# Two diffusion trunk layers: three of the four norms leave the input of the matmul and go to its output, and GpSimd splits each weight tile in two halves

## The reference

```
def rmsnorm(x, g):      return x * rsqrt(mean(x * x, axis=-1) + EPS) * g
def adaln(cvec, w, b):  return split(silu(cvec) @ w + b, 6)
def modulate(x, g, shift, scale):
    return rmsnorm(x, g) * (1 + scale) + shift
def conv_ffn(h, w_up, conv_w, conv_b, w_down):
    u = dwconv_centered(h @ w_up, conv_w, conv_b)
    g, v = split(u, 2)
    return (silu(g) * v) @ w_down
h = modulate(x, norm_mix_g, shift, scale);  x = x + gate * mixer(h)
h = modulate(x, norm_ffn_g, shift, scale);  x = x + gate * conv_ffn(h, ...)
```

## Time and profile before

| | us |
|---|---|
| median of 3 runs (range) | 2111.81 (2111.33 to 2116.29) |
| profiled execution, its own time | 2114.69 |
| its span | 2112.9 |
| mean granted clock of PE, share of full | 0.954 |

### The profile page before, as it was taken

How to read it: one execution, slowest core, us unless ns; L and a number is a source line. 1 busy time by engine, 2 the same in 40 slices (tenths; PEclk the granted TensorE clock), 3 DMA queues, 4 the chain that set the end, 5 groups by cost and what they waited for, 6 DMA issues and landing times. The chain is left out here.

```text
span 2112.9 us, 32465 instructions
## 1 busy us (share of the span) xinstructions
PE 1954.0 (92%) x12945; PEld 1826.9 (86%) x12945; DVE 1022.0 (48%) x1456; ACT 582.7 (28%) x1046; POOL 1123.4 (53%) x437
## 2 busy tenths in 40 slices
PE   5799888899999999997999999987897999999997
PEld 3688777789999899997998989976896999999997
DVE  2545673454414432537467676668315451452343
ACT  2233330121101110213365655655102210220121
POOL 2223324445575567764544445432474777776763
PEclk8799998899999999998999999988898999999999
DMA  9321118645525222222333333311421222222211
GB/s 285 103 60 40 36 37 265 184 142 181 161 82 182 91 60 76 66 77 90 103 118 93 97 116 98 110 60 50 130 70 40 79 70 70 79 69 71 79 55 75
DMA packets 293060, 208.78 MB, mean 99 GB/s; under 512 B 7480, under 2 KB 285021, under 8 KB 292445
## 3 DMA queue, kind: packets, MB, share of 16 engines
q1 hardware_dynamic: 292957, 207.32, 32.2%
HBM read 196.63 MB, written 10.67 MB: 98 GB/s over the span
## 5 line engine op out<-in xcount | busy, mean ns | idle before, releaser
L825 POOL TENSOR_SCALAR w_hi<-raw 128x1024 fp32r<-128x1024 f32 (+1 forms) x216 | 607.9, 2814 | 945.3 <-PE ps L856 870.6
L856 PE MATMUL ps<-h_hi,w_hi 128*128 128x322 f32 (+1 forms) x2304 | 560.5, 325 | 22.0 <-DVE h_lo L1679 22.0
L856 PE MATMUL ps<-h_lo,w_hi 128*128 128x322 f32 (+1 forms) x2304 | 533.2, 313 | 0.0
L856 PE MATMUL ps<-h_hi,w_lo 128*128 128x322 f32 (+1 forms) x2304 | 532.3, 312 | 0.0
L828 POOL TENSOR_TENSOR w_lo<-raw,w_hi 128x1024 fp32r<-128x1024 f32 (+1 forms) x216 | 515.1, 2385 | 18.0
L856 PEld LDWEIGHTS ps<-h_hi,w_hi 128*128 128x128 f32 x2304 | 391.8, 192 | 51.3 <-issue 34.0
L856 PEld LDWEIGHTS ps<-h_hi,w_lo 128*128 128x128 f32 x2304 | 393.5, 191 | 0.0
L856 PEld LDWEIGHTS ps<-h_lo,w_hi 128*128 128x128 f32 x2304 | 391.7, 191 | 0.0
L856 PE MATMUL ps<-g_hi,w_hi 128*128 128x322 f32 (+1 forms) x816 | 191.1, 316 | 10.2 <-DVE g_lo L1923 10.2
L856 PE MATMUL ps<-g_lo,w_hi 128*128 128x322 f32 (+1 forms) x816 | 189.4, 314 | 0.0
L856 PE MATMUL ps<-g_hi,w_lo 128*128 128x322 f32 (+1 forms) x816 | 188.8, 313 | 0.0
(11 more groups left out here) (291 smaller groups left out, 2208.5 us busy)
## 6 DMA issues: line engine op xcount, KB each, us to landing
ada<-in_ada_w SPq DMA_DIRECT2D x48, 1024.0 KB, 5.9
raw<-in_ffn_w_up SPq DMA_DIRECT2D x88, 512.0 KB, 3.8
raw<-in_ssd_w_in SPq DMA_DIRECT2D x40, 512.0 KB, 4.0
R<-scr_acs SPq DMA_DIRECT2D x40, 512.0 KB, 4.8
raw<-in_ffn_w_down SPq DMA_DIRECT2D x32, 512.0 KB, 4.1
raw<-in_att_w_in SPq DMA_DIRECT2D x16, 512.0 KB, 5.9
raw<-in_ssd_w_out SPq DMA_DIRECT2D x16, 512.0 KB, 4.2
raw<-in_ffn_w_down SPq DMA_DIRECT2D x16, 384.0 KB, 3.4
```

Of the source, the lines that this page charges most:

```text
L825: nc.gpsimd.tensor_scalar(w_hi[j % 2][:, 0:k, :], raw[j][:, 0:k, :], 1.0, None, ALU.mult).then_inc(w_hi_done, 1)
L856: ins = mm(out[:, cols], w[slot][:, k, :], x[:, k_of(k), cols], start=first and k == 0 and i == 0, stop=last and k == n - 1 and i == 2)
```

## The change

Four edits.

1. For norms 0, 1 and 3 the root leaves h. `high` and `low` write h_hi = round(x·gain) and h_lo = x·gain − h_hi straight behind each residual, with no root in them. Since the root is one number per token (a column of the tile), it is multiplied into the accumulator when a tile is evicted: `root_row` and `row` put it into a row buffer (`rbs`, `rrow_att`), and `scale` multiplies a whole MLP tile in place in PSUM; in attention the multiplication is the copy to SBUF itself. The shift goes into the two columns that were zero, now side by side (`PADS`): the matmul turns them into W·shift, and ACT adds that as a bias. In the MLP, `side_pads` copies them to the tile's borders for the outer taps, and a small operation forms the biases. `ss` and `norm_rb` stand inside the first two tiles behind the norm.
2. Norm 2 (state-space) stays as it was.
3. POOL makes each weight tile with four instructions, two halves of `w_hi` and two halves of `w_lo`, instead of two.
4. The modulation steps come in another column order (`ADA_ORDER`), so that gains come first; the last ones of the attention output are done two tiles earlier. h of norm 3 has its own memory (`h2_a` to `h2_d`), since its old place still holds the state-space output. The residual loop behind the state-space mixer is unrolled.

```diff
-                pool.wait_ge(w_hi_done, t + 1)
-                nc.gpsimd.tensor_tensor(w_lo[j % 2][:, 0:k, :], raw[j][:, 0:k, :], w_hi[j % 2][:, 0:k, :].bitcast(F32),
-                                        ALU.subtract).then_inc(w_split, 1)
+                cuts = ((0, k // 2), (k // 2, k))
+                for a_, b_ in cuts:
+                    nc.gpsimd.tensor_scalar(w_hi[j % 2][:, a_:b_, :], raw[j][:, a_:b_, :], 1.0, None, ALU.mult
+                                            ).then_inc(w_hi_done, 1)
+                for n_, (a_, b_) in enumerate(cuts):
+                    pool.wait_ge(w_hi_done, 2 * t + (1 + n_))
+                    ins = nc.gpsimd.tensor_tensor(w_lo[j % 2][:, a_:b_, :], raw[j][:, a_:b_, :],
+                                                  w_hi[j % 2][:, a_:b_, :].bitcast(F32), ALU.subtract)
+                ins.then_inc(w_split, 1)
...
+                            begins = peeled and p == 0
+
+                            def row(k, half=half):
+                                if half == 0 and k == 5:
+                                    ss(n_)
+                                if half == 1 and k == 3:
+                                    norm_rb(n_)
+
+                            steps(half, half, h_of(n_), range(KD), ready=h_wait(n_) if begins and half == 0 else None,
+                                  after=row if begins else None).then_inc(mm_done, 1)
                             if ada:
                                 s = 2 * i + (s0 + half)
...
+            def high(n, k):
+
+
+                act.wait_ge(gain_done, k // 2 + 1 + 4 * n if n < 2 else 7 + n)
+                hi, _ = h_at_k(n, k)
+                for s_, cols in SEGS:
+                    ins = A_(hi[:, cols], xT[:, k, cols], ACT.Copy, scale=gain1[:, n, k, s_:s_ + 1])
...
-                            A_(buf[:, :], acc(half), ACT.Identity, bias=param_at(m + bcol),
-                               scale=param_at(m + (wc + 44))).then_inc(ffn_id, 1)
+                            for s_, cols in ((0, slice(0, S0)), (1, slice(S0, W))):
+                                b_ = 24 + 2 * half + s_
+                                ins = A_(buf[:, cols], acc(half)[:, cols], ACT.Identity, bias=small[:, b_:b_ + 1],
+                                         scale=param_at(m + (wc + 44)))
+                            ins.then_inc(ffn_id, 1)
...
+            def low(n, k):
+
+                dve.wait_ge(gain_done, k // 2 + 1 + 4 * n if n < 2 else 7 + n)
+                dve.wait_ge(h_hi_done, 8 * n + k + 1)
+                hi, lo = h_at_k(n, k)
+                for s_, cols in RANGES:
+                    ins = stt(lo[:, cols], xT[:, k, cols], gain1[:, n, k, s_:s_ + 1], f32(hi[:, cols]), ALU.mult,
+                              ALU.subtract)
+                    (step(ins) if s_ == 0 else ins.then_inc(h_ready, 1))
+
...
+            def root_row(n):
+
                 inv_root(n)
-                if n in (0, 3):
-                    h_zeros()
                 tt(diag[:, :, :], bc(ident, 1, CHUNKS), bc(small[:, 48:53], 2, P), ALU.mult).then_inc(diag_done, 1)
+
+            def row(n):
+
+                if n:
+                    step(nc.vector.memset(rrow(n)[:, PADS], -1.0))
...
-                        low(k - 1)
-                low(KD - 1)
+                for s_, cols in RANGES:
+                    step(cp(rrow(n)[:, cols], bank(4, P) if s_ == 0 else bank(5)))
+                step.wait()
+
+            def scale(slot, n):
+
+                step(tt(acc(slot), acc(slot), rrow(n)[:, :], ALU.mult))
+                step.wait()
+
+            def side_pads(slot):
+
+                step(cp(acc_wide(slot)[:, 0:W + 2:W + 1], acc(slot)[:, PADS]))
 
...
                         continue
-                    if t >= 12:
+                    src = acc(t % 2)
+                    if t < 12:
+                        h, i = divmod(t, 3)
+                        dve.wait_ge(mm_done, t + 1)
+                        if t == 0:
+                            dve.wait_ge(x_spilled, 16)
+                            row(0)
+                        if h and i == 1:
+                            dve.wait_ge(*att_end(("trk", h - 1)))
+                        if h and i == 2:
+                            dve.wait_ge(*att_end(("trv", h - 1)))
+                        tt((q_raw, k_raw, v_raw)[i][:, :], src, rrow_att[:, :], ALU.mult).then_inc(acc_free_dve, 1)
+                        if t == 0:
+                            att_zeros()
...
@@ -1904,11 +2052,19 @@
                     def pair(i, ada):
                         for half, buf in enumerate((cg, cv)):
                             m = i + (m0 + FT * half)
+                            dve.wait_ge(mm_done, 2 * i + (tp + half + 1))
+                            if isinstance(i, int) and (p, i, half) == (0, 0, 0):
+                                row(n_)
+                            scale(half, n_)
+                            side_pads(half)
+                            nw = nws[:, m:m + 1] if isinstance(m, int) else nws[:, bass.ds(m, 1)]
+                            ts(small[:, 24 + 2 * half:26 + 2 * half], acc(half)[:, PADS], nw, pcol_at(m + bc_), ALU.mult,
+                               ALU.add).then_inc(ffn_v, 1)
                             dve.wait_ge(ffn_id, 2 * i + (2 * f0 + half + 1))
...
+            for m in range(KD):
+                dve.wait_ge(mm_done, T_O + 4 * (m // 2) + 2 + m % 2 + 1)
+                buf = tn[m % 2]
+                for s_, cols in RANGES:
+                    ins = stt(buf[:, cols], acc(m % 2)[:, cols], modc(1, 2, m, s_), rbs[:, cols], ALU.mult, ALU.mult)
+                    (step(ins) if s_ == 0 else ins.then_inc(acc_free_dve, 1))
+                dve.wait_ge(acc_free_dve, dve_accs(A_O) + m)
+                for s_, cols in RANGES:
+                    ins = tt(xT[:, m, cols], xT[:, m, cols], buf[:, cols], ALU.add)
+                    (step(ins) if s_ == 0 else ins.then_inc(so_x, 1))
+                dve.wait_ge(so_x, m + 1)
+                if m:
+                    low(3, m - 1)
+                if m >= 2:
+                    add_square(3, m - 1, sq[(m - 1) % 2])
             add_square(3, 7, sq[1])
-            norm(3)
+            low(3, 7)
+            dve.wait_ge(shift_hi, 4)
```

More of the change, by code:

```diff
@@ L262, in build @@
         wdt_lo = fixed("wdt_lo", [P, KD, 64], F32R)
+        dtb_bc = fixed("dtb_bc", [P, 64])
+        a_bc = fixed("a_bc", [P, 64])
         early_end = top[0]
@@ L358, in build @@
         xdt = a("xdt", [P, 2, 512])
-        xw = [a(f"xw{i}", [P, 512]) for i in range(2)]
+        xw_1 = a("xw1", [P, 512])
         st_b = a("st_b", [P, 4, 512])
@@ L643, in _ @@
                 load(t, t, w_att[:, :, att_col(t):att_col(t) + P])
-            for s in range(5, 9):
+            for s in range(5, 8):
                 ada(s)
@@ L846, in _, with steps @@
             mm, tr = nc.tensor.matmul, nc.tensor.transpose
-            def steps(t, slot, aslot, x_hi, x_lo, ks, k_of=lambda k: k, first=True, last=True, n=KD, ready=None):
+            def steps(slot, aslot, x_of, ks, first=True, last=True, n=KD, ready=None, after=None):
                 out = acc(aslot)
@@ L1050, in _ @@
                     begin(T_B + m, A_B + m)
-                    steps(T_B + m, m % 2, m % 2, g_hi, g_lo, range(KD)).then_inc(mm_done, 1)
+                    steps(m % 2, m % 2, g_of, range(KD)).then_inc(mm_done, 1)
                 for s in ADA_B[m]:
@@ L1098, in down @@
                             ready = (lambda k: pe.wait_ge(f_ready, FT * l + m0 + k + 1)) if peeled and half == 0 else None
-                            steps(t, half, half, g_hi, g_lo, range(n), n=n, ready=ready).then_inc(mm_done, 1)
+                            steps(half, half, g_of, range(n), n=n, ready=ready).then_inc(mm_done, 1)
                     down(0, True)
@@ L1118, in y_part @@
                         pe.wait_ge(*acc_free(A_O + half - 2))
-                    ins = steps(None, half, half, y_hi, y_lo, (k % KD,), k_of=lambda _: k, first=part == 0,
-                                last=part == 1)
+                    ins = steps(half, half, y_of(part), (k % KD,), first=part == 0, last=part == 1)
                     if k % KD == KD - 1:
@@ L1263, in so_pair @@
                             pe.wait_ge(acc_free_dve, 2 * i + (half + dve_accs(A_O) - 2))
-                        steps(None, half, half, y_hi, y_lo, range(KD), k_of=lambda k: 8 * part + k, first=part == 0,
-                              last=part == 1).then_inc(mm_done, 1)
+                        steps(half, half, y_of(part), range(KD), first=part == 0, last=part == 1).then_inc(mm_done, 1)
             for k in range(12, 16):
@@ L1482, in _ @@
             ffn(0, T_F0, T_F0)
-            norm(2)
+            root(2)
+            for k in range(KD):
+                act.wait_ge(t_done, k + 1)
+                for s_, cols in SEGS:
+                    ins = A_(h_hi[:, k, cols], tn[k % 2][:, cols], ACT.Identity, bias=modc(1, 0, k, s_))
```

(17 more changed lines are left out.)

409 lines of the change are left out of this document (234 added, 175 removed).

## The result

The changed kernel takes 2078.04 us (median of 4 runs, 2075.3 to 2081.86) against 2111.98 in the same rounds: a ratio of 0.9834, with a 95% interval from 0.9815 to 0.9853 (the ratio is the recorded one; the two medians alone give 0.9839, inside the interval). The profiled execution took 2075.3 of its own time against 2114.69, with a span of 2073.5 instead of 2112.9: 39.4 less, where I had forecast 38.6.

A forecast was written before the change was run, and what follows sets the result against it. PE was taken as the bound, busy 1954.0 of 2112.9 us. The terms -16.3, -15.7, -11, +2.6, +1.5, +1.3 and -1 sum to -38.6: 2114.7 becomes 2076.1, median 2073, range 2060 to 2088.

The forecast's parts named there:

- Norm 3: Behind the state-space output: PE's third tile starts at T+20.8 (T: last tile's end) instead of 37.1, -16.3 us.
- Norm 1: Behind the attention output: PE's third tile starts at T+19.1 (T: last tile's end) instead of 34.8, -15.7 us.
- Norm 0: At the kernel's start: the second tile is done at 76.5 us instead of 87.6, -11 (7 to 12).
- MLP eviction: MLP loops: DVE's chain frees the slot at 12.9 us, PE wants it at 14.2; 0 over 44 pairs.
- g_lo: Last pair ahead of a down-projection: g_lo, which PE awaits, comes 0.5 us later; five waits, +2.6.
- Attention: Attention: 12 tiles evicted by DVE and biased by ACT, bounds 0 and +14, taken as +1.5 us; halved splits change nothing.
- State-space: Two splits each 0.5 us longer and three small instructions ahead of the first residual, +1.3; shorter DVE waits on w_lo, -1.
- The signs: Expected waits: sums about 12 us, h_lo about 6; clock near 1.0 behind norms 1 and 3; scale 0.8 to 0.9.
- attention on the path: Rival: all 12 attention evictions stay on PE's path, +14 us instead of +1.5, giving 2085; chance 0.12.
- the late waits: Rival: squares and last low part come a whole w_lo later at each norm; gains 12, 12, 7, giving 2085; chance 0.09.
- More is won: Rival: state-space and attention gain 4 us each from shorter locks, the start 12, giving about 2063; chance 0.12.
- The slow one: Rival: DVE bounds the MLP if scale costs over 0.65 us more; at 2.3 each, 2140 us; chance 0.04.

The follow-up runs named there:

- The repetition: The changed kernel run again as it is, no edit, in the same rounds as the other runs: 2080.49 us, 0.9834 of the kernel before.

## Why the prediction held, point by point

- **Norm 3** (-16.3) won 18.1. The sums were 1.2 less late (wait 0.49, not 1.7), since the additions ran beside w_lo's two halves, 2.65 us for the pair (with whole splits the wait is 1.36), and the slot wait was 1.7, not 2.
- **Norm 1** (-15.7): the third tile at T+18.2, forecast 19.1. The rest of the 18.8 in the table is mostly the modulation work that has moved.
- **Norm 0** (-11): 11.2. DVE reads the first step out at 34.49 instead of 38.88, 4.4 earlier (forecast 3.7), and the column sums take 2.3 of it back; but PE then waits 1.1 for the weights of a step and 0.9 for DVE, which I had not priced, and the last turn starts only 0.3 earlier (56.60 against 56.94). Tile 0 starts at 58.42 where I had 58.8.
- **MLP eviction** (0 in the loops) held, with its chain: evicted at 4.6 (forecast 4.6), hm at 6.3 (6.5), g_lo at 8.6 (8.3), slot free at 13.2 (12.9). The scale takes 0.831 on average, 0.89 forecast. What the step left out is the new memory of h: rows of 648 cost 1.9 us.
- **The median**: the profiled execution was forecast within 0.8 us (2076.1, measured 2075.3). The median is 5 above the 2073 given, because I took it to lie 2.9 below the profiled execution, as in the kernel before; here it lies 2.7 above. That is a matter of which execution was profiled, and no mechanism.
- **g_lo** (+2.6): the waits rose by 1.2 only; the clock took 6.0 us behind them against 3.0 before, which I had not priced. The repetition, with the same waits, lost 2.5, so this is chance.
- **Attention** (+1.5) failed in its sign: 5.8 are won by v and 7.3 by the first output matmul in this execution. The eviction by DVE, for which the +1.5 stood, costs PE no wait (12.4 us of standing still before and after). "DVE and POOL take turns and end at about the same time, so nothing" failed: the halves take 1.7 us out of PE's waits in both kernels. The other 4 us up to v are PE's busy time, that is the clock, and vary by as much between executions of the same code.
- **State-space** (+1.3 and -1): +1.3 from the last MLP residual (-28.2) to the last state-space residual (-27.0), where the sum had 0.3. The two waits for w_lo rose by 2.0 (8.9 to 10.9); that shorter locks would win 1 back does not show, since PE stands still for 2 us more with halves in this part.
- **Left out altogether:** SP's order at the attention output. I had read the diff's `ada(8)` behind `g_ready` and costed nothing; PE waits there 10.5 us instead of 1.5, and that took more than attention had won. And the last turn of the modulation, 5.3 us won, which I had put into "another column order".
- **The signs.** Scale at 0.83, hm at 1.6 (I had 1.8), the clock of 1.00 behind both norms and no wait on scale or taps inside the loops came as written. For the waits I had given about 12 on the sums and about 6 on h_lo, and 6.9 and 3.3 came: norm 2's own wait for h_lo was 3.3 already before, not 6, and on the sums only 6.4 belong to the norms that did not change.

The rivals: attention on the path and the late waits did not come. "More is won" gave attention and state-space 4 each from shorter locks: in PE's waits attention won 1.7 and state-space lost 2, and the sum did not come. The slow one is further away than I wrote: DVE has 1.8 us of cover per pair, not 1.3. The total was close because +9.0 (DMA order), +1.9 (rows) and +3.0 (clock) stand against -9 in attention and -5.3 (the turn), none of them in the sum: the mechanisms of the three norms were right, the precision of the sum was luck.

The lock rule (the Trainium skill, "SBUF — State Buffer", Who interferes with whom), which the page states not for any GpSimd operation but for one that reads SBUF, as w_hi's does, would have g_lo wait for the whole first half of w_hi that starts with it: 1.49 and its own 0.83. Here g_lo starts at 1664.60, 0.02 behind that half, and takes 1.27, so it lost 0.44: more than the nothing that I had taken from the earlier trace rows, less than the rule says. The scale at 1665.80, which reads one operand from PSUM, runs inside the same pair of w_hi in 0.82, undelayed. The earlier trace rows was thin ground: that addition overlaps w_hi for its last 0.27 us alone. The kernel before has better rows:

```profile
278.76 2.77 POOL L825 TENSOR_SCALAR w_hi<-raw 128x1024 fp32r<-128x1024 f32 x1 [17.23 <-PE ps L856]
...
278.90 1.57 DVE L1859 TENSOR_TENSOR g_lo<-pmul,g_hi 128x642 fp32r<-128x642 f32 x1 [0.81 <-ACT g_hi L1409]
...
1565.07 2.78 POOL L825 TENSOR_SCALAR w_hi<-raw 128x1024 fp32r<-128x1024 f32 x1 [1.83 <-PE ps L856]
...
1567.03 0.82 DVE L1666 TENSOR_TENSOR sums<-sums,sq 128x642 f32<-128x642 f32 x1
```

A product that starts 0.14 behind w_hi takes 1.57 instead of 0.83. Sixteen additions in that profile start 1.0 to 2.0 us behind a w_hi and run inside it to their end, and all take 0.82. So in these rows w_hi holds such an instruction up only near its own start.

## What to carry to other kernels

A factor that is one number per column of the output can leave the input and go into the eviction; what it wins is the chain and the clock behind it, 11 to 18 us a norm here. In the MLP loops it cost no time, where the evicting chain of 13.2 us stayed under the 14.3 of two tiles; where no tile covers it, at the start of a phase and ahead of a down-projection, PE waited for it. When a change gives an old buffer a new tenant, look at what used to be loaded into it early, and at the order of the queue behind the point where it comes free: the bytes in front of a small transfer are its wait. Two remedies for the same wait (starting later, a shorter lock) do not add; test each alone on the kernel before and on top of the other. And split a gain into waiting and busy time before giving it a cause: here 4 us of busy time came and went with the clock in code that nobody had touched.

## What the runs showed of the hardware

- Behind PE's waits ahead of the down-projections the clock fell in 23 of 39 cases for waits of 1.79 to 3.83 us, each time for 1.0 to 1.5 us of a tile and once for 2.5, and in different ones from execution to execution of one kernel; for waits of up to 1.62 it never fell, 21 of 21.
- A matmul of 320 or 322 columns took 0.1474 us with the rows of its input 642 elements apart and 0.1484 with them 648 apart, at the same clock.
- DVE multiplies 642 columns from PSUM to PSUM in 0.83 us, 88 of them in a mean of 0.831 and none above 0.84, with POOL at work beside each; a product of two SBUF tiles that starts with POOL's subtraction takes 2.95 instead of 0.83. One that starts with POOL's w_hi is held up by 0.44 (half a tile's w_hi) to 0.74 (a whole one), one that starts at least 1.0 us behind it not at all.
